# A transformer block and two mixer layers on one core: activation tables held, sums and halves re-placed around the even and odd layers, 17 convolution taps on TensorE

## The reference, cut to what matters

```
x = x + 0.5*gt1*swiglu(modulate(rms_norm(x)))        # ffn 1, hidden width 2816
x = x + gt2*hybrid_mixer(modulate(rms_norm(x)))      # mLSTM (4 heads) beside dilated attention (8 heads)
x = x + 0.5*gt3*swiglu(modulate(rms_norm(x)))        # ffn 2
x = rms_norm(x, g_final)
# even layer
h = rms_norm(x, even_norm);  u_pool, u_ssm, z = split(h @ w_in)
y = concat(multiscale_pool(u_pool), glu(s5(u_ssm) @ w_glu)) * silu(z);  x = x + y @ w_out
# odd layer
h = rms_norm(x, odd_norm);  val, gt, z = split(h @ w_in, 3)
c = causal_conv_31_taps(val * sigmoid(gt)) + conv_b          # each of 1024 channels by itself
c = (c - mean(c)) * rsqrt(var(c) + 1e-5) * ln_g + ln_b       # mean and var over the channels
x = x + (silu(c) * silu(z)) @ w_out
return rms_norm(x, final_norm)
```

## Time and profile before

| | us |
|---|---|
| median of three runs | 1755.61 (1755.4 to 1758.85) |
| the profiled execution | 1755.22 |
| its span, first to last instruction | 1753.3 |
| PE busy in it | 1603.1 |
| DVE busy | 896.0 |
| ACT busy | 642.4 |
| POOL busy | 367.5 |

### The profile page before, as it was taken

How to read it: one execution, slowest core, us unless ns; L and a number is a source line. 1 busy time by engine, 2 the same in 40 slices (tenths; PEclk the granted TensorE clock), 3 DMA queues, 4 the chain that set the end, 5 groups by cost and what they waited for, 6 DMA issues and landing times. The chain is left out here.

```text
span 1753.3 us, 18533 instructions
## 1 busy us (share of the span) xinstructions
PE 1603.1 (91%) x6791; PEld 1190.3 (68%) x6791; DVE 896.0 (51%) x1240; ACT 642.4 (37%) x923; POOL 367.5 (21%) x469
## 2 busy tenths in 40 slices
PE   4899999998999998889899999999999989988367
PEld 3788888886774554234688888888777768766246
DVE  4777246335533334444453434432645445899844
ACT  3422212223334542443343212222521234666544
POOL 3011000000000000001000578720001100699900
PEclk9899999999999998669999999999999999999779
DMA  9777435322321111000323243364132123222101
GB/s 343 231 260 267 149 107 169 95 90 76 93 64 36 36 36 60 1 0 18 97 85 98 90 147 96 97 217 138 50 107 91 55 75 97 72 74 83 48 24 48
DMA packets 203731, 176.34 MB, mean 101 GB/s; under 512 B 6907, under 2 KB 183367, under 8 KB 203142
## 3 DMA queue, kind: packets, MB, share of 16 engines
q1 hardware_dynamic: 188438, 121.87, 23.5%
q0 software_dynamic: 14064, 51.34, 8.3%
q10 hardware_dynamic: 1152, 2.10, 0.3%
HBM read 166.90 MB, written 8.39 MB: 100 GB/s over the span
## 5 line engine op out<-in xcount | busy, mean ns | idle before, releaser
L1860 PE MATMUL ps<-h_hi,w_hi 128*128 128x512 f32 x1224 | 492.8, 403 | 29.7 <-DVE w_lo L1172 14.5
L1861 PE MATMUL ps<-h_lo,w_hi 128*128 128x512 f32 x1224 | 482.1, 394 | 0.0
L1862 PE MATMUL ps<-h_hi,w_lo 128*128 128x512 f32 x1224 | 481.9, 394 | 0.0
L1172 DVE TENSOR_TENSOR w_lo<-w_stage,w_hi 128x1024 fp32r<-128x1024 f32 x225 | 298.7, 1341 | 232.0 <-ACT w_hi L749 229.7
L1860 PEld LDWEIGHTS ps<-h_hi,w_hi 128*128 128x128 f32 x1224 | 233.0, 190 | 105.5 <-issue 53.8
L749 ACT ACTIVATE w_hi<-w_stage 128x1024 fp32r<-128x1024 f32 x225 | 230.9, 1048 | 195.4 <-PE ps L1862 188.0
L1862 PEld LDWEIGHTS ps<-h_hi,w_lo 128*128 128x128 f32 x1224 | 232.9, 190 | 50.3
L1861 PEld LDWEIGHTS ps<-h_lo,w_hi 128*128 128x128 f32 x1224 | 233.4, 191 | 46.7 <-issue 0.7
L1860 PE MATMUL ps<-a_hi,w_hi 128*128 128x512 f32 x544 | 214.4, 394 | 19.3 <-DVE a_lo L1798 12.8
L1861 PE MATMUL ps<-a_lo,w_hi 128*128 128x512 f32 x544 | 213.1, 392 | 0.0
L1862 PE MATMUL ps<-a_hi,w_lo 128*128 128x512 f32 x544 | 212.8, 391 | 0.0
(11 more groups left out here) (406 smaller groups left out, 1627.4 us busy)
## 6 DMA issues: line engine op xcount, KB each, us to landing
w_stage<-in_w_gu SPq DMA_DIRECT2D x88, 512.0 KB, 4.3
ada_w<-in_w_ada POOLq DMA_DIRECT2D x72, 512.0 KB, 6.3
w_stage<-in_w_down SPq DMA_DIRECT2D x44, 512.0 KB, 3.7
w_stage<-in_w_in SPq DMA_DIRECT2D x24, 512.0 KB, 3.8
w_stage<-in_odd_w_in SPq DMA_DIRECT2D x24, 512.0 KB, 3.7
w_stage<-in_even_w_in SPq DMA_DIRECT2D x16, 512.0 KB, 3.8
w_stage<-in_w_out SPq DMA_DIRECT2D x8, 512.0 KB, 4.0
mats<-mats_d POOLq DMA_DIRECT2D x4, 1024.0 KB, 7.2
```

What stands on the lines that cost most here:

```text
L1172: dve.tensor_tensor(w_lo[:, c % RING], w_in[:, c % RING], w_hi[:, c % RING].bitcast(F32), ALU.subtract).then_inc(w_split, 1)
L1860: pe.matmul(bank, w_hi[:, slot, k], rhs_hi, start=start, stop=False, skip_group_check=True)
L1861: pe.matmul(bank, w_hi[:, slot, k], rhs_lo, start=False, stop=False, skip_group_check=True)
L1862: return pe.matmul(bank, w_lo[:, slot, k], rhs_hi, start=False, stop=stop, skip_group_check=True)
```

## The change

- A load of the table set that holds both Ln and Exp stands ahead of the mLSTM. 24 table loads leave ACT's program, which has 45 before and 21 now: 15 net in the mLSTM, 8 in the attention, 1 in the odd layer. The load ahead of the odd layer's Ln is placed before the last square.
- End of ffn 2 and even layer: the running sum for the even norm is added by POOL (`even_added`). PE begins the even layer five `xT` tiles sooner, and does the norm sums at k = 6. The normalising of `xT` (`final_rows`) moves behind the first takes, two tiles in each of steps 1 to 4. PE no longer waits for tile 1 at n = 2. `rows_by_chunk` stands behind the projection.
- GLU: the halves have buffers of their own (`y_hi` over `mats`, `y_lo` over `us`) and are made from step 13 on.
- Even output: the first two output tiles take k = 0 to 6 first, and k = 7 of both behind.
- Odd layer: tiles 6 and 7 have 8 and 9 taps on PE, as float32 products with diagonal matrices `dgc` (17 ACT copies of 128 x 128, in steps 6 to 14). POOL has 11 and 8 taps of them, DVE 11 and 13; tiles 0 to 5 keep 13 and 17.
- Odd layer norm: a shift `m0n` (minus the channel mean of tile 0 alone) is added to every tile, in tiles 2 to 7 through the first DVE tap. Squares of the shifted tiles are taken as the tiles are finished (`square_of`) and summed on PE (`spread`); the variance is the mean square less the square of the mean. The mean is subtracted tile by tile in the last loop (`deviate`).
- The weight halves T_OOUT+2 and +3 are made before the factor is there, on both engines.

The diff, cut to its core:

```diff
-POOL_TAPS = 13
+PE_TAPS = [0] * 6 + [8, 9]
+POOL_TAPS = [13] * 6 + [11, 8]
+DVE_TAPS = [TAPS - 1 - p - q for p, q in zip(POOL_TAPS, PE_TAPS)]
...
@@ gpsimd, even_mixer
+                for kt in range(1, KT - 1):
+                    pool.wait_ge(sq_ready, squares(N_EVEN, kt))
+                    upto(pool, even_added, kt - 1)
+                    pool.tensor_tensor(tmp[:, 0], tmp[:, 0], sq[:, 1], ALU.add).then_inc(even_added, 1)
@@ scalar, two_squares and mlstm
-                    act.wait_ge(sq_added, added(N_EVEN, kt - 1))
+                    act.wait_ge(sq_added, added(N_FIN, kt - 1))
+                    act.wait_ge(even_added, kt - 1)
+                act.preload_act_table_set("natural_log_exp_and_others")
                 decay(0)
@@ scalar, even_mixer
+                    if n >= 13:
+                        y_half(n - 13)
+                y_half(3)
                 pool_hi(3)
-                for t in range(4):
-                    y_hi(t)
@@ scalar, odd_mixer
+                    if n == 9:
+                        act.wait_ge(mean_sum, 1)
+                        act.activation(m0n[:], ps[6][:], ACT.Copy, scale=-1.0 / P).then_inc(m0_ready, 1)
+                    for u in range(KT - 2):
+                        if n == (10 + u if u < 2 else 3 * u + 7):
+                            square_of(u)
...
+                    if 6 <= n < 6 + len(PE_OF) // 2 + 1:
+                        for m in range(2 * (n - 6), min(2 * (n - 6) + 2, len(PE_OF))):
+                            u, k = PE_OF[m]
+                            act.activation(dgc[:, m], ident[:], ACT.Copy, scale=cw[:, u, k:k + 1]).then_inc(dgc_ready, 1)
...
+                square_of(KT - 2)
+                for n in range(2):
+                    hi(0, T_OOUT + 2 + n)
+                act.preload_act_table_set("natural_log_exp_and_others")
+                square_of(KT - 1)
+                act.wait_ge(mean_sum, 1 + KT)
+                act.wait_ge(var_sum, KT - 1)
+                act.activation(lsq[:, 0], ps[6][:], ACT.Square, scale=1.0 / D).then_inc(lr_ready, 1)
+                act.activation(m0n[:], ps[6][:], ACT.Copy, scale=-1.0 / D).then_inc(m0_ready, 1)
@@ vector
-            add_square(N_EVEN, kt - 1)
...
-                for kt in range(KT):
+                def final_rows(kt):
                     dve.scalar_tensor_tensor(xT[:, kt], xT[:, kt], cols[:, G_FINAL + kt:G_FINAL + kt + 1], tmp2[:, 0],
...
+                    if 1 <= n <= 4:
+                        final_rows(2 * n - 2)
+                        final_rows(2 * n - 1)
...
+                    if n >= 14:
+                        y_lo_of(n - 14)
...
+                        link(dve.tensor_tensor(cv[:, t], pacc[:, t % 2], ps[t - 6][:], ALU.add))
+                        link(dve.tensor_tensor(cv[:, t], cv[:, t], ps[4][:], ALU.add))
+                        dve.tensor_tensor(cv[:, t], cv[:, t], ps[5][:], ALU.add).then_inc(cv_ready, 1)
...
-                for t in range(KT):
-                    dve.scalar_tensor_tensor(cv[:, t], ps[6][:], -1.0 / D, cv[:, t], ALU.mult, ALU.add) \
-                        .then_inc(cc_ready, 1)
+                for n in range(2):
+                    lo(0, T_OOUT + 2 + n)
+                dve.scalar_tensor_tensor(lsq[:, 0], ps[7][:], 1.0 / D, lsq[:, 0], ALU.mult, ALU.subtract).then_inc(lr_ready, 1)
+                for t in range(2):
+                    link(deviate(t))
@@ tensor
+                if norm_after == N_ODD:
+                    for part in (range(KT - 1), [KT - 1]):
+                        for n in range(2):
...
-                pe.wait_ge(x_new, X_FFN[1] + 2 * KT - 1)
+                pe.wait_ge(x_new, X_FFN[1] + KT + 3)
...
-                            if k == 4:
+                            if k == 6:
                                 norm_total(N_FIN, 0, rs[:])
                                 norm_total(N_EVEN, 1, tmp[:, 0]).then_inc(sq_used, 1)
...
-                        pe.wait_ge(even_read, 2)
...
+                    if n == 3 * KT - 2:
+                        pe_taps(KT - 2)
+                spread(KT - 3)
+                pe_taps(KT - 1)
                 mean(KT - 2)
+                spread(KT - 2)
                 mean(KT - 1)
```

More of the change, by code:

```diff
@@ L83, with of_tiles @@
 TAPS = 31
-POOL_TAPS = 13
+PE_TAPS = [0] * 6 + [8, 9]
+POOL_TAPS = [13] * 6 + [11, 8]
+DVE_TAPS = [TAPS - 1 - p - q for p, q in zip(POOL_TAPS, PE_TAPS)]
+PE_OF = [(t, 1 + POOL_TAPS[t] + j) for t in range(8) for j in range(PE_TAPS[t])]
+def of_tiles(taps, t):
+    return sum(taps[:max(t, 0)])
 MH, AH, DH = 4, 8, 64
@@ L340, in build_program @@
         o_rows = put("o_rows", [P, ST, D])
+        put = region(at_of["a_lo"] + 2 * S * 4, 6 * S * 4)
+        dgc = put("dgc", [P, sum(PE_TAPS), P])
+        put = region(at_of["a_hi"] + KT * S * 4, 3 * S * 4)
+        lsq = put("lsq", [P, 2, S])
+        m0n = put("m0n", [P, S])
         mats_d = nc.dram_tensor("mats_d", [4, P, SEC, MAT * P], F32).ap()
@@ L896, in project_posts @@
                         act.wait_ge(g_chain, 11)
-                        act.activation(exp_m[:], fm_g, ACT.Exp, scale=-1.0).then_inc(em_ready, 1)
+                        act.activation(exp_m[:], fm_g, ACT.Exp, scale=-1.0).then_inc(lsig, 1)
             def mlstm():
@@ L1692, in even_mixer @@
                             .then_inc(mix_ready, 1)
-                for t in range(4):
-                    y_lo(t)
                 for q in range(4):
```

193 lines of the change are left out of this document (121 added, 72 removed).

## The result

| | before | after |
|---|---|---|
| median, us | 1755.51 (4 runs, 1750.84 to 1758.85) | 1729.64 (4 runs, 1728.14 to 1731.69) |
| profiled execution, us | 1755.22 | 1730.85 |
| its span, us | 1753.3 | 1729.0 |

The changed kernel is faster by 1.45%: ratio 0.9855, 95% interval 0.983 to 0.9881. The forecast was 1713 with a range of 1703 to 1727, so the gain came out at 25.9 us instead of 42.5, and the time 2.6 us above the range. PE's busy time hardly moved, 1607.6 us now against 1603.1, so the gain is idle time: 121.4 us of the span now, 150.2 before. The forecast had counted some 13 us of it as busy time at a higher clock.

What follows compares the result with a forecast made beforehand. PE, busy 91% of the span, was taken as the bound, losing time in waits (longest at the odd layer's end) and half-clock stretches. Terms -20.4 - 3.8 - 10 + 0 - 8.3 + 0 = -42.5 gave 1713 us, range 1703 to 1727.

Steps and rivals of the forecast that it cites:

- Part 2: Attention: three waits ahead of spreads each shrink by 1.28, -3.8 us; two half-clock stretches run at full clock, -10 us.
- no fall behind a wait under 1.6: Attention: no clock fall seen behind waits under 1.6 us mid-program, so waits of 1.2 should leave two stretches at 2.4 GHz.
- Rival (a): Attention: the clock falls all the same, so part 2 is only -3.8 and the time 1723 us; 22%.
- Part 4: End of ffn 2 and even layer's start: waits and half clock -6.6, later sums +1.1, turns +5.6; sum 0 us.
- Rival (c): Even start at its bad end, turn waits in full and a clock fall ahead of the sums: 1718 us; 15%.
- Part 1: Odd layer's end: tile 7 ready 7.5 us earlier, shorter steps behind its sum, loop additions costed at nothing; -20.4 us.
- Part 3: GLU and even output: shorter or filled waits and no half clock behind them; -8.3 us.
- rival (d): Each table load also drains ACT, so three attention waits vanish and the odd end wins 1.4: 1709 us; 4%.
- (e): Odd loop locks, with ACT's squares, DVE's merge and POOL's adds waiting on each other: slower, 1764 us; 3%.

Runs made afterwards that it cites:

- a_probe: Changed kernel with PE's four sums over the heads' squares in the attention reading a constant, so the reference is not computed: 1721.71 us, ratio 0.9815.
- a_fill: Changed kernel with six products that nobody reads put into PE's waits in the attention: 1722.54 us, ratio 0.9825.
- a_head: Changed kernel with the spreads and sums for the mLSTM's heads moved behind the turn in each attention step: 1712.80 us, ratio 0.9742.
- a_turns: Changed kernel with the even stage's turn into rows back in its old place ahead of the step's projection: 1722.40 us, ratio 0.9808.
- a_evenbuf: Changed kernel with the squares of the even stage's norm alternating between two buffers: 1722.72 us, ratio 0.9817.
- a_nope: Changed kernel without taps on PE, 13 on POOL and 17 on DVE for every tile: 1735.23 us, ratio 0.9867.
- a_noshift: Changed kernel without subtracting tile 0's mean in the odd layer norm's sums: 1722.15 us, ratio 0.9807.

## Why the prediction was wrong

**Part 2, the clock in the attention, is the step that failed**: -10 forecast, -1.1 measured (the stage is 5.4 us shorter, and 4.3 of that is idle time). The waits did what they were to (1.06, 0.12, 1.06 for 1.2, 0.3, 1.2). The error was to tie each fall to the one wait just ahead of it, and to take "no fall behind a wait under 1.6" as a rule: in the changed kernel the clock falls right behind both waits of 1.06 (at 720.6 and 761.6). The stage had five stretches at half clock and 14.4 us of idle time spread over 131; removing 4.3 of it left the falls, and only a_probe, a_fill and a_head, at 8.0, 7.4 and 6.6, have clearly fewer us at half clock. Rival (a), at 22%, named this outcome and its reason; it should have been as likely as the forecast. The mechanism, clock for idle time, was right: one edit of order later it paid 16.7 us (20.2 less 3.5).

**Part 4, the even start**: 0 forecast, +4.8 measured. The turns cost 5.1 (by a_turns) for 5.6; the removed waits and POOL's adds together came to -0.3 for -6.6 + 1.1 = -5.5. What failed is the term for POOL's adds: I took 1.26 to 1.47 us for an add from the odd loop's rows, and it took 1.85, so a tile took 3.26 for my 2.6 to 2.8, 3 to 4 us over six tiles; PE waited 4.21 for the sums and fell to half clock in that wait, at 1256.5. The second buffer (a_evenbuf) gives 4.4 back. My row was of adds beside taps that read PSUM. Rival (c), 15%, named the turns and the fall, and its size.

**Part 1, the odd layer**: -20.4 forecast, -17.5 measured. Tile 7 was ready 7.3 us earlier by the taps (7.5 forecast). Of this 0.6 is lost again ahead of its sum: a_nope takes 48.7 us from the loop's last row in the table to that sum, the kernel before 48.1, and without the shift (a_noshift) 0.5 comes back. Behind the sum the steps took 11.5 us for the 11.9 forecast. The mis-sized term is the loop, costed at 0 with 1.4 as the most: it cost 2.3. I had counted the two early subtractions (the loop's first step lost 1.4) and overlooked that the first tap of each later tile, a plain scaling before, now reads m0n as a second SBUF operand: 1.55 for 0.70 us, 0.3 us more for each tile.

**Part 3**: -8.3 forecast, -7.0 measured. The even output's 4.3 for 4.4 is right. The GLU's waits came to 1.57 in pieces (1.3 forecast); its 96 products stand 0.233 us apart now where they stood 0.227 apart, which makes 0.6, for a reason that stays open; the last 0.4 I cannot place.

Add 0.8 for the start and the mLSTM, and the parts' misses make 2.9 + 8.4 + 1.3 + 4.8 + 0.8 = 18.2 us, the 1730.85 of the profiled run against my 1712.7.

The table load was taken at 1.28, and the waits fell by 1.43, 1.42 and 1.42. The two long ones did not vanish, so rival (d) is out. The loop did not lock (e): ACT's squares cost it nothing.

## What to carry to other kernels

Where a stage has several stretches at half clock, sum its idle time over the stage, and do not count on the clock for removing one wait next to it. Try moving independent work into the waits first: that order was worth 16.8 us in the median on the changed kernel, though only 4.7 on the kernel before, whose waits were longer. Price an elementwise instruction by a row with the same operands (SBUF or PSUM) and the same neighbour on the other engine, and look at every instruction that gains an operand. And compare traces instruction by instruction: single runs of one kernel scattered by up to 13 us here, while the attention repeated within 0.2 us in six traces with the same stretches at half clock.
